# Gate and up rows in plain order, a small item's rows gathered once, and item ends moved into the next item's loop

## The reference

```python
logits = (xf @ router_w).astype(jnp.float32)
top_vals, top_idx = lax.top_k(logits, TOP_K)            # 2 of 8
top_w = jax.nn.softmax(top_vals, axis=-1)
gates = jnp.sum(jax.nn.one_hot(top_idx, N_EXPERTS) * top_w[..., None], axis=1)
for e in range(N_EXPERTS):
    y = y + gates[:, e:e + 1] * ((silu(xf @ w_gate[e]) * (xf @ w_up[e])) @ w_down[e])
```

## Time and profile before

| | us |
|---|---|
| median of 3 runs | 1548.97 |
| lowest, highest | 1548.1, 1549.16 |
| the profiled execution | 1547.38 |
| its span, first to last instruction | 1545.7 |

### The profile page before, as it was taken

How to read it: one execution, slowest core, us unless ns; L and a number is a source line. 1 busy time by engine, 2 the same in 40 slices (tenths; PEclk the granted TensorE clock), 3 DMA queues, 4 the chain that set the end, 5 groups by cost and what they waited for, 6 DMA issues and landing times.

```text
span 1545.7 us, 19875 instructions
## 1 busy us (share of the span) xinstructions
PE 1420.8 (92%) x7640; PEld 1201.6 (78%) x7640; DVE 1181.4 (76%) x941; ACT 997.4 (65%) x798; POOL 82.9 (5%) x82
## 2 busy tenths in 40 slices
PE   7967899999878969999899999989999999999997
PEld 6956899999878857787677887767887677888666
DVE  5795455453768567989989898997988988887996
ACT  5765343342368347658976767886767887775894
POOL 0574000000022000000000000000000000000000
PEclk9976999999988979999999999999999999999999
DMA  9510355455334749999999998998999999999990
GB/s 300 164 55 0 109 165 165 151 172 167 99 119 150 270 191 366 330 363 346 410 390 331 370 358 335 406 403 318 363 370 336 394 409 335 345 365 329 392 364 29
DMA packets 148538, 426.41 MB, mean 276 GB/s; under 512 B 6624, under 2 KB 64608, under 8 KB 134112
## 3 DMA queue, kind: packets, MB, share of 16 engines
q1 hardware_dynamic: 148448, 425.11, 75.1%
HBM read 424.04 MB, written 1.05 MB: 275 GB/s over the span
## 4 chain that ended last, share of the span: by engine, by line
PE 62%; DVE 13%; ACT 10%; issue 7%; ACTq 0%; DVEq 0%
PE P L1462 45%; ACT whi L829 5%; DVE over_gates_lo L1211 4%; PE P L1802 4%; PE P L1803 4%; PE P L1827 3%; DVE raw_lo L1211 3%; PE P L1717 2%; PE P L1731 1%; ACT whi L617 1%; ACT hb L923 1%; DVE xbf L1171 1%; PE P L1762 1%; DVE acc L1365 1%; PE P L1551 1%
## 5 line engine op out<-in xcount | busy, mean ns | idle before, releaser
L1211 DVE TENSOR_TENSOR raw_lo<-raw,whi 128x2048 fp32r<-128x2048 f32 x168 | 374.6, 2283 | 14.5 <-ACT whi L829 14.3
L1211 DVE TENSOR_TENSOR over_gates_lo<-over_gates_raw,whi 128x2048 fp32r<-128x2048 f32 x144 | 322.6, 2285 | 19.6 <-ACT whi L829 18.9
L829 ACT ACTIVATE whi<-raw 128x2048 fp32r<-128x2048 f32 x168 | 312.2, 1912 | 26.7 <-PE P L1462 26.7
L829 ACT ACTIVATE whi<-over_gates_raw 128x2048 fp32r<-128x2048 f32 x144 | 265.6, 1911 | 7.5 <-DMA over_gates_raw<-in_moe_w_gate 7.5
L1462 PE MATMUL P<-hn_hi,whi 128*128 128x272 f32 (+1 forms) x640 | 188.3, 294 | 15.6 <-DVE hn_lo L977 13.6
L956 DVE TENSOR_TENSOR raw_lo<-raw,whi 128x2048 fp32r<-128x2048 f32 (+3 forms) x72 | 152.2, 2137 | 64.8 <-ACT whi L617 64.8
L1802 PE MATMUL P<-whi,xe_hi 128*128 128x512 f32 x448 | 183.9, 410 | 13.5 <-DVE over_gates_lo L1211 6.6
L1462 PE MATMUL P<-whi,xe_hi 128*128 128x512 f32 x448 | 180.4, 403 | 7.9 <-DVE over_gates_lo L1211 5.6
L1462 PE MATMUL P<-hn_hi,raw_lo 128*128 128x272 f32 (+1 forms) x640 | 186.7, 292 | 0.0
L1462 PE MATMUL P<-hn_lo,whi 128*128 128x272 f32 (+1 forms) x640 | 186.4, 291 | 0.0
L1462 PE MATMUL P<-whi,xe_lo 128*128 128x512 f32 x448 | 177.1, 395 | 0.0
(11 more groups left out here) (274 smaller groups left out, 2526.6 us busy)
## 6 DMA issues: line engine op xcount, KB each, us to landing
raw<-in_moe_w_up SPq DMA_DIRECT2D x64, 1024.0 KB, 6.2
raw<-in_moe_w_gate SPq DMA_DIRECT2D x64, 1024.0 KB, 5.9
over_gates_raw<-in_moe_w_down SPq DMA_DIRECT2D x64, 1024.0 KB, 6.2
over_gates_raw<-in_moe_w_gate SPq DMA_DIRECT2D x48, 1024.0 KB, 6.1
raw<-in_moe_w_down SPq DMA_DIRECT2D x40, 1024.0 KB, 7.2
over_gates_raw<-in_moe_w_up SPq DMA_DIRECT2D x32, 1024.0 KB, 6.2
over_xb_raw<-in_moe_w_up SPq DMA_DIRECT2D x16, 1024.0 KB, 6.2
raw<-in_w_in_even SPq DMA_DIRECT2D x10, 1024.0 KB, 10.7
```

The costliest lines, as they stand in the source:

```text
L829: act.activation(whi[u % HI][:, :], moe_raw[k % MOE_RAW][:, :], ACT.Copy).then_inc(hi_ready, 1)
L1211: dve.tensor_tensor(moe_lo(k), moe_raw[k % MOE_RAW][:, :], whi[u % HI][:, :].bitcast(F32), ALU.subtract).then_inc(lo_ready, 1)
```

## The change

It does three things. First, the rows `silu` and `hb` are written in plain order, and PE reads its tiles by stride (`tile_of`: a tile takes every n-th element of a row, 32 bytes apart, or 16 in the last step), as stationary operand of the turn and fold matmuls. Second, the gather of a small item computes 64 columns instead of 128, and the low part of the token rows is taken from the same 64 columns. Third, where a small item follows a large one or a large one a small one, the last step's turn or fold is done after the split of unit 1 of the next item (`ROWS_AT` = 1), the token rows after the split of unit 2 (`XE_AT` = 2), and ACT's copy of the finished output after the split of unit 5 (`FINISH_AT` = 5) instead of unit 2. Only item 7 keeps its own end. PE's order of work is unchanged.

```diff
+ROWS_AT, XE_AT, FINISH_AT = 1, 2, 5
-        def by_partition(t, n):
-            return t[:, 0:128 * n].rearrange("t (j p) -> t p j", p=128)
-        def in_order(x, n):
-            return x.rearrange("t (p j) -> t p j", j=n)
+        def tile_of(rows, n, j):
+            return rows[:, 0:128 * n].rearrange("t (p j) -> t p j", j=n)[:, :, j]
...
# ACT
+            def rows_high(i, b):
+                if b is None:
+                    turn_high(i, STEPS - 1)
+                else:
+                    silu_folded(i, STEPS - 1)
+                    folded_high(i, STEPS - 1)
...
             def small(i, b, last):
                 for k in range(PER_ITEM):
                     split_item_hi(i, k)
-                    if k == 2:
+                    if k == ROWS_AT:
+                        rows_high(after_item(i, -1), None)
+                    if k == XE_AT:
+                        xe_high(i, True)
+                    if k == FINISH_AT:
                         finish(after_item(i, -1))
...
-                            act.activation(by_partition(silu, n), in_order(wide(0, s), n), ACT.Copy).then_inc(g_copied, 1)
+                            act.activation(silu[:, 0:WIDTHS[s]], wide(0, s), ACT.Copy).then_inc(g_copied, 1)
...
-                            act.activation(by_partition(hb, n), in_order(wide(2, s), n), ACT.Copy).then_inc(u_copied, 1)
+                            act.activation(hb[:, 0:WIDTHS[s]], wide(2, s), ACT.Copy).then_inc(u_copied, 1)
...
-                silu_folded(i, STEPS - 1)
-                folded_high(i, STEPS - 1)
-                xe_high(after_item(i, 1), False)
+                if last:
+                    rows_high(i, b)
+                    xe_high(after_item(i, 1), False)
# DVE
-                    dve.tensor_tensor(xe_hi[:, :, SMALL:CHUNK], x[:, :, SMALL:CHUNK], xe_hi[:, :, 0:SMALL].bitcast(F32),
+                    dve.tensor_tensor(xe_hi[:, :, SMALL:CHUNK], x[:, :, 0:SMALL], xe_hi[:, :, 0:SMALL].bitcast(F32),
...
+            def rows_low(i, was_small):
+                if was_small:
+                    fold_product(i, STEPS - 1)
+                    folded_low(i, STEPS - 1)
+                else:
+                    turn_low(i, STEPS - 1)
...
-                            dve.tensor_tensor(by_partition(hb, n), in_order(silu[:, 0:WIDTHS[s]], n),
-                                              in_order(wide(2, s), n), ALU.mult).then_inc(h_ready, 1)
+                            dve.tensor_tensor(hb[:, 0:WIDTHS[s]], silu[:, 0:WIDTHS[s]], wide(2, s), ALU.mult)\
+                                .then_inc(h_ready, 1)
...
+                    if k == ROWS_AT:
+                        rows_low(after_item(i, -1), False)
+                    if k == XE_AT:
+                        xe_low(i, True)
...
# PE
-            def gather(i):
+            def gather(i, n):
...
-                        last = pe.matmul(P[:, 6 + k // 4, 128 * (k % 4):128 * (k % 4) + 128],
-                                         xs[:, c, 128 * k:128 * k + 128], sel_m[:, c], start=c == 0, stop=c == 1)
+                        last = pe.matmul(P[:, 6 + k // 4, 128 * (k % 4):128 * (k % 4) + n],
+                                         xs[:, c, 128 * k:128 * k + 128], sel_m[:, c, 0:n], start=c == 0, stop=c == 1)
...
-                    last = pe.matmul(turn_banks(s)[:, 128 * n:128 * n + 128], hb[:, 128 * n:128 * n + 128],
+                    last = pe.matmul(turn_banks(s)[:, 128 * n:128 * n + 128], tile_of(hb, tiles, n),
...
-                        last = pe.matmul(dst[:, SMALL * n:SMALL * n + SMALL], rows[:, 128 * n:128 * n + 128], fold[:, :],
+                        last = pe.matmul(dst[:, SMALL * n:SMALL * n + SMALL], tile_of(rows, tiles, n), fold[:, :],
```

More of the change, by code:

```diff
@@ L875, in large @@
                         split_item_hi(i, k)
-                    if k == 2 and not first:
+                    if after_small is not None:
+                        if k == ROWS_AT:
+                            rows_high(after_item(i, -1), after_small)
+                        if k == XE_AT:
+                            xe_high(i, False)
+                        if k == FINISH_AT:
+                            finish(after_item(i, -1))
+                    elif k == 2 and not first:
                         finish(after_item(i, -1))
@@ L888, in large @@
                         sel_turned(i)
-                turn_high(i, STEPS - 1)
-                xe_high(after_item(i, 1), next_small)
+                if not next_small:
+                    rows_high(i, None)
+                    xe_high(after_item(i, 1), False)
             def silu_folded(i, s):
@@ L1376, in next_sel, with large @@
                 make_sel(after_item(i, 1), small)
-            def large(i, first, next_small):
+            def rows_low(i, was_small):
[4 more added lines that the diff above has]
+                    turn_low(i, STEPS - 1)
+            def large(i, first, next_small, after_small=False):
                 for k in range(PER_ITEM):
@@ L1381, in large @@
                         split_item_lo(i, k)
+                    if after_small and k == ROWS_AT:
+                        rows_low(after_item(i, -1), True)
+                    if after_small and k == XE_AT:
+                        xe_low(i, False)
                     if first and k == 8:
@@ L1423, in folded_low, with small @@
                                   pair_of[:, :, 0:SMALL].bitcast(F32), ALU.subtract).then_inc(ht_ready, 1)
-            def small(i):
+            def small(i, last):
                 for k in range(PER_ITEM):
                     split_item_lo(i, k)
+                    if k == ROWS_AT:
+                        rows_low(after_item(i, -1), False)
+                    if k == XE_AT:
+                        xe_low(i, True)
                     done = k - LAG
@@ L1437, in small @@
                         next_sel(i, False)
-                fold_product(i, STEPS - 1)
-                folded_low(i, STEPS - 1)
-                xe_low(after_item(i, 1), False)
+                if last:
+                    rows_low(i, True)
+                    xe_low(after_item(i, 1), False)
             large(0, True, True)
             with dve.Fori(0, (NE - 2) // 2) as p:
-                small((p, 1))
-                large((p, 2), False, True)
-            small(NE - 1)
+                small((p, 1), False)
+                large((p, 2), False, True, after_small=True)
+            small(NE - 1, True)
             dve.wait_ge(head_ready, 2)
@@ L1760, in turn @@
                     pe.wait_ge(ht_ready, nth(i, STEPS, s))
-                for n in range(WIDTHS[s] // 128):
-                    last = pe.matmul(turn_banks(s)[:, 128 * n:128 * n + 128], hb[:, 128 * n:128 * n + 128],
+                tiles = WIDTHS[s] // 128
+                for n in range(tiles):
+                    last = pe.matmul(turn_banks(s)[:, 128 * n:128 * n + 128], tile_of(hb, tiles, n),
                                      cst("ident"), is_transpose=True, start=True, stop=True)
@@ L1778, in large_down, with large @@
                     last.then_inc(unit_used, 1)
-            def large(i, first):
+            def large(i, first, next_small):
                 pe.wait_ge(xe_ready, nth(i, 1, 1))
@@ L1796, in large @@
                 turn(i, STEPS - 1)
-                gather(after_item(i, 1))
+                gather(after_item(i, 1), SMALL if next_small else CHUNK)
                 large_down(i, STEPS - 1)
@@ L1858, in small @@
                 fold_rows(i, b, STEPS - 1)
-                gather(after_item(i, 1))
+                gather(after_item(i, 1), CHUNK)
                 small_down(i, STEPS - 1)
             pe.wait_ge(fold_ready, 1)
-            gather(0)
-            large(0, True)
+            gather(0, CHUNK)
+            large(0, True, True)
             with pe.Fori(0, (NE - 2) // 2) as p:
                 small((p, 1), p)
-                large((p, 2), False)
+                large((p, 2), False, True)
             small(NE - 1, (NE - 2) // 2)
```

21 lines of the change are left out of this document (11 added, 10 removed).

## The result

The changed kernel takes 1596.09 us (median of 4 runs, 1595.53 to 1599.53) against 1549.07 before (1548.1 to 1549.24): a ratio of 1.0311, 95% interval 1.0298 to 1.0324. It is 47 us slower. The prediction was 1533, with 1526 to 1593 as its range; the time lies just above that, where the rival of slow strided loads put it (1587 to 1597).

What follows compares the result with a forecast made beforehand. PE was taken to bound large items, DVE to pace small ones. Gains of 2.9 (item 1), 4.4 each (3, 5), 3.8 (7) and 0.5 (gathers), together 16.0 us, gave 1531.4 profiled, 1533 as median; range 1526 to 1593.

Steps and rivals of the forecast that it cites:

- the rival of slow strided loads: PE's fold and turn loads cost 0.107 to 0.128 us more each: +38 to +49 us, 1587 to 1597; chance 0.42.
- Strided tiles on PE: Fold and turn loads by stride: between zero and 0.128 us more per load; zero taken.
- first sign of being wrong: Small items' folds on PE: the prediction fails first if one takes over 4.5 us.
- The rest of the walk: Step-by-step timing of copies, gathers, item ends and clock through the items, 16.0 us gained in all.
- Copies: Plain copies on ACT save 1.0 us on each of six and half on two, 7 us per small item.
- Item ends, large to small: DVE splits units 0 and 1 in idle time; down(3) not late, cover left 0.7 us.
- Item ends, small to large: down(3) starts 1.5 to 1.6 us late, large item waits too; of 3.8 us gained 2.9 remain.
- The gather: Four gathers compute 64 columns; the load sets the pace, 0.12 us saved each, 0.5 us in all.
- Clock: Wait ahead of down(2) shrinks to about 2.3 us; items 3 and 5 freed of 1.54 us clock loss each.
- DMA: Rival: if 384 GB/s is the limit, small items keep their length, 1544 us; chance 0.06 together with held rows.
- The chances: Whole kernel: forecast 0.48, held rows or DMA 0.06, half-way price 0.04, slow loads 0.42.

Runs made afterwards that it cites:

- e11: Kernel before with plain copies and fold tiles read at a stride of three elements, small items only (output not right): 1577.4 us.
- e8: Changed kernel with sorting on the PSUM read and plain tiles for PE, item ends moved, small items gathered once: 1527.9 us, 1529.78 when run again.
- e4: Kernel before with the sorting moved to ACT's and DVE's read of PSUM, SBUF written in runs, plain tiles for PE: 1534.47 us.
- e2: Kernel before with only the item ends moved into the next item's loop, rows sorted by the writer, full gathers: 1543.55 us.
- e3: Changed kernel with the strided tiles undone: item ends moved, small items gathered once, rows sorted by the writer: 1542.15 us.
- e7: Kernel before with plain copies and strided tiles in small items only, fold matmuls with 128 moving columns in place of 64: 1595.03 us.
- e12: Kernel before with plain-order rows and strided tiles in large items alone (turns), small items as before: 1549.23 us.
- e1: Kernel before with only plain-order rows and strided tiles in folds and turns, gathers and item ends as before: 1605.0 us.

## Why the prediction was wrong

**The step that failed** is the choice in "Strided tiles on PE": zero for a cost with two ends, 0 and 0.128 us a load. A fold's load went from 0.110 to 0.234 us, +0.124, at the upper end, and a fold from 3.52 to 7.49 us, past the 4.5 us that the prediction named as its first sign of being wrong. The argument for zero was that the scatter draws a moving operand at 2.4 elements per ns where a load asks for 1.2. It fails twice. The scatter is 8 records of 512 columns, as its line shows, not of 1024: 4096 columns in 3.43 us are 1.2 per ns, the load's own pace.

```profile
824.23 3.60 PE L1731 MATMUL P<-ys,sel_t 128*128 128x512 f32 x8
```

The matmuls 0.235 us apart do draw 512 columns each, 2.2 per ns, but that compares the wrong things: they take four neighbours from each line of 16 bytes, 0.55 lines per ns, and the load by stride asks for one line per element, 1.2 per ns. Worked in lines no row is evidence for slack; e11 and the changed kernel show 0.55 to 0.58 lines per ns as what a fold's load gets. The rule of the Trainium skill was right here, for folds. So was the size taken from the strided write, 0.128 us; that a write of ACT and a load of PE cost nearly the same is not shown to be more than a coincidence.

**The rest of the walk held.** e8 is the forecast with the load at zero: 1527.9 and 1529.78 us against 1533. Predicted were 16.0 us, measured 17.3 in length and 20.9 in the medians (18.2 the second time), which differ also ahead of the experts. By items, with each large item counted to the small one before it: 3.4 for the predicted 2.9 (item 1), 4.9 and 4.7 for 4.4 (items 3 and 5), 4.4 for 3.8 (item 7).
- Copies: 1.0 us less each, as counted; 1.03 us. e4 gained 9.6 us of length.
- Item ends, large to small: DVE's idle time went as walked, and no wait of PE ahead of a large item's down(3) appeared.
- Item ends, small to large: a wait of 1.5 to 1.6 us ahead of down(3) was predicted, 1.44 measured; PE's second wait, predicted 1.0, was 0.74. In the changed kernel itself PE does not wait ahead of down(3), as the fold ends later there.
- The ends by themselves bring 4.6 us of length (e2): 0.6 us on a pair whose clock had held, about 2 on the two others by taking up the clock loss. Sorting on the PSUM read alone brings 9.6 (e4), both and the gather together 17.3.
- The gather: 0.5 predicted, 0.4 measured between e2 and e3, not to be told from zero.
- Clock: the wait ahead of down(2) shrank to 2.33 us, 2.3 predicted, but items 3 and 5 were counted as freed of the loss by it, 3.1 us, and that was not so: in e8 items 1 and 5 lost the clock behind this same wait, 3 and 7 kept it. Where it was lost, the large item behind was 1.5 us shorter, since the new waits took the loss up. So the 3.1 us came, by another way than was said: luck.
- DMA did not take over: at 108.66 us item 3 of e8 drew 390 GB/s, and no split waited for a transfer on ACT or DVE.

**The rival was right in its load and near in its total, with two terms that work against each other.** It priced 448 fold loads at 0.107 to 0.128 us, 48 to 57 us; e7 less e4 is 55.8 us. It added 10 to 12 us for the turns; e12 shows none. And it did not have the clock behind each fold, 14.9 us by e1 less e7. So it has the small items at 28 to 37 us net where 56.5 were measured, and the large ones at +10 to +12 where they got 2.7 us shorter. Its +38 to +49 holds the 47 us between the medians but not the 53.8 of items 1 to 7; in the profiles the changed kernel reached the experts 3.7 us earlier than before, on unchanged code, so that the total came so close is in part luck. Against e8 the changed kernel loses 71.1 us (890.8 - 819.7), and e1 less e4, the same exchange without the item ends, is 70.7: the load's 55.8 and the clock's 14.9.

**The chances.** 0.48 against 0.42 for two ends of a cost that no row priced was a guess between them; the only price in the trace, and the page of the Trainium skill, pointed one way.

## What to carry to other kernels

Count a strided stationary operand in 16-byte lines, not elements: in float32, two elements per line were nearly free in a fold and one doubled the load, and where loads set PE's pace there is nothing to hide it in. (The transposes of a turn did not pay; try before you count on either.) If rows have to be sorted for PE, do it in the engine that copies PSUM to SBUF, on its read side: it was free on ACT and DVE, while the same sort on the write side doubled a copy on ACT. Before giving an unpriced cost the value zero, look for the row that would be the worst case, and ask in its units.

## What the runs showed of the hardware that was not expected

- The granted clock fell to 1.2 GHz in and behind folds in which the trace shows PE without idle time: 32 strided load records with matmuls of 64 columns in 7.49 us. With 128 columns, in 7.44 us, and with 64 plain load records in 7.1 us, it stayed at 2.4 GHz.
- The same stride of 32 bytes left a turn's pace as it was (eight transposes 1.05 us for 1.04), and took a fold's load from 0.110 to 0.234.
- ACT and DVE read PSUM at a stride of 32 bytes at full pace: 1024 columns in 1.02 and 1.22 us. Written to SBUF at 512 bytes' distance the same copy took 2.03 us.
